# An eighth 2 MB weight slot for the experts, two output buffers instead of three, one buffer of gathered rows, and two reused slots loaded by halves

## The reference, cut to what matters

```python
# router: each token takes the 2 best of 8 experts of the best of 8 groups (64 experts)
order = jnp.argsort(eid)                      # 1024 assignments, sorted by expert
hid = jax.nn.silu(xb @ w1[e]) * (xb @ w3[e])  # w1, w3: 1024 x 512 in f32, 2 MB each
y   = hid @ w2[e]                             # w2: 512 x 1024 in f32, 2 MB
y_assign = y_slots[dest] * s_gate[:, None]    # each row by its gate, summed by token
```

## Time and profile before

| | |
|---|---|
| runs | 3236.83, 3237.40, 3237.57 us; median 3237.4 |
| profiled execution | span 3237.6 us from first to last instruction; the time of the runs is this same quantity, with nothing to add around it |
| PE busy / DVE / ACT / POOL | 95% / 43% / 28% / 6% of the span |
| mean granted clock of TensorE | 0.985 of full speed |
| HBM read / written | 600.30 MB / 18.90 MB |
| experts' loads on SP's queue | 7 names of slots, 2048 KB each, first issued at 2212.9 us, last at 3179.9 us |

### The profile page before, as it was taken

How to read it: one execution, slowest core, us unless ns; L and a number is a source line. 1 busy time by engine, 2 the same in 40 slices (tenths; PEclk the granted TensorE clock), 3 DMA queues, 4 the chain that set the end, 5 groups by cost and what they waited for, 6 DMA issues and landing times.

```text
span 3237.6 us, 35048 instructions
## 1 busy us (share of the span) xinstructions
PE 3082.8 (95%) x14831; PEld 2160.6 (67%) x14831; DVE 1377.5 (43%) x2276; ACT 890.4 (28%) x1429; POOL 194.1 (6%) x182
## 2 busy tenths in 40 slices
PE   9999999999999999999999999999999999999996
PEld 7668688887667778888888787888443344344342
DVE  5675543335486553333767665534311111111112
ACT  3453332232244332222244442322111111111111
POOL 0000000000000000000211010000100000000000
PEclk9999999999999999999999999999999999999998
DMA  5122222333222222323222121134999999999997
GB/s 181 53 79 91 66 91 89 101 108 121 66 66 91 79 77 86 104 93 115 86 85 69 62 98 59 59 104 166 406 429 430 430 431 429 429 430 430 430 429 304
DMA packets 192100, 611.07 MB, mean 189 GB/s; under 512 B 13396, under 2 KB 130932, under 8 KB 166976
## 3 DMA queue, kind: packets, MB, share of 16 engines
q1 hardware_dynamic: 177440, 585.65, 46.4%
q10 hardware_dynamic: 9056, 18.83, 1.7%
q0 software_dynamic: 5440, 4.27, 0.4%
HBM read 600.30 MB, written 18.90 MB: 191 GB/s over the span
## 4 chain that ended last, share of the span: by engine, by line
PE 84%; DVE 9%; ACT 3%; issue 2%; DMA 2%; POOL 1%; ACTq 0%; SPq 0%; POOLq 0%; DVEq 0%
PE bank L123 81%; PE bank L126 3%; DVE gate_acc L141 2%; DMA highs<-in_moe_w 1%; DVE probs L144 1%; DVE aprobs L144 1%; DVE x_tok L141 1%; ACT probs L129 1%; DVE qs L138 1%; DVE piece_rounded L138 0%; POOL root L138 0%; ACT piece_high_rounded L129 0%; DVE stat L156 0%; DVE small L135 0%; ACT xT_low_rounded L129 0%
## 5 line engine op out<-in xcount | busy, mean ns | idle before, releaser
L138 DVE TENSOR_TENSOR piece_rounded<-piece,piece_high_rounded 128x2048 fp32r<-128x2048 f32 (+2 forms) x160 | 346.8, 2171 | 526.3 <-ACT piece_high_rounded L129 526.1
L123 PE MATMUL bank<-xT_rounded,piece_high_rounded 128*128 128x512 f32 (+1 forms) x1424 | 542.0, 381 | 9.6 <-DVE piece_rounded L138 4.9
L123 PE MATMUL bank<-xT_low_rounded,piece_high_rounded 128*128 128x512 f32 (+1 forms) x1424 | 539.2, 379 | 0.0
L123 PE MATMUL bank<-xT_rounded,piece_rounded 128*128 128x512 f32 (+1 forms) x1424 | 539.0, 379 | 0.0
L138 DVE TENSOR_TENSOR gate_and_hidden<-gate_and_hidden,bank 64x512 f32<-64x512 f32 x64 | 69.2, 1082 | 762.4 <-ACT gate_and_hidden L129 762.4
L129 ACT ACTIVATE piece_high_rounded<-piece 128x2048 fp32r<-128x2048 f32 (+2 forms) x160 | 288.1, 1804 | 254.5 <-DMA piece<-in_ffn_w_down 102.4
L123 PEld LDWEIGHTS bank<-xT_rounded,piece_high_rounded 128*128 128x128 f32 x1424 | 270.0, 190 | 61.7 <-DVE piece_rounded L138 5.5
L123 PEld LDWEIGHTS bank<-xT_rounded,piece_rounded 128*128 128x128 f32 x1424 | 270.0, 190 | 49.2
L123 PEld LDWEIGHTS bank<-xT_low_rounded,piece_high_rounded 128*128 128x128 f32 x1424 | 270.0, 190 | 48.5
L123 PE MATMUL bank<-xT,xeT 128*64 128x512 f32 x496 | 237.2, 634 | 58.4 <-issue 57.9
L123 PE MATMUL bank<-tail_pair,xeT 128*64 128x512 f32 x512 | 244.9, 634 | 0.5 <-DVE extra L135 0.5
(11 more groups left out here) (350 smaller groups left out, 4832.1 us busy)
## 6 DMA issues: line engine op xcount, KB each, us to landing
tail_pair<-in_moe_w SPq DMA_DIRECT2D x32, 2048.0 KB, 21.8
highs<-in_moe_w SPq DMA_DIRECT2D x32, 2048.0 KB, 21.8
piece_high<-in_moe_w SPq DMA_DIRECT2D x31, 2048.0 KB, 17.3
xT<-in_moe_w SPq DMA_DIRECT2D x31, 2048.0 KB, 17.4
mT_pair<-in_moe_w SPq DMA_DIRECT2D x22, 2048.0 KB, 22.6
pieces<-in_moe_w SPq DMA_DIRECT2D x22, 2048.0 KB, 22.7
memory_norms<-in_moe_w SPq DMA_DIRECT2D x21, 2048.0 KB, 22.8
piece<-in_ffn_w_in SPq DMA_DIRECT2D x40, 1024.0 KB, 4.9
```

The costliest lines, as they stand in the source:

```text
L123: return self.engine.matmul(*a, **k) if self.engine is not None else Nothing()
L138: return self.engine.tensor_tensor(*a, **k) if self.engine is not None else Nothing()
```

## The change

`OUTS` goes from 3 to 2 and `rows` from two buffers to one. A slot `low`, released by the last gate product of the retention's merge, is put ahead of `tail`, so that eight pieces have a slot of their own (`FIRST_PIECES`). The pieces that take the first two reused slots, p8 and p9, are loaded by `load_first_reused`: the first halves of both when PE has done half of expert 0's upper products, the second halves when it has done the rest. Small tables of the router move to other places: `picks`, `rank`, `wide`, `both` and `local` to where `outs` and `ehidT` will be, so `out_act(0)` and `out_act(1)` wait for the mark `slots 1`; `e15` (and the slots' table in it) goes behind `xeT`.

```diff
-OUTS = 3
+OUTS = 2
+FIRST_PIECES = 8
...
-WORK = 119 * 256
+WORK = 120 * 256 + 32
...
         carve_from(0)
         self.outs = [carve(f"outs{j}", BANK) for j in range(OUTS)]
         self.ehidT = [carve(f"ehidT{j}", EH // P, CAP) for j in range(2)]
+        self.both, self.local = (carve(n, NT, EXPERTS) for n in ("both", "local"))
...
-        self.rows = [carve(f"rows{j}", D) for j in range(2)]
+        self.rows = carve("rows", D)
...
-        carve_from(WORK - 2 * SLOT)
+        carve_from(WORK - 4 * SLOT)
+        self.low_pair = carve("low_pair", 2 * SLOT)
         self.tail_pair = carve("tail_pair", 2 * SLOT)
...
+    def load_first_reused(self, e, n):
+
+        halves = []
+        for piece in (n, n + 1):
+            name, _, marks = self.slots[piece]
+            to, w, rows = self.expert_piece(piece), self.plan[piece][1], self.piece_rows(piece) // 2
+            halves.append((piece, f"piece_{name}_landed", marks, to, w, rows))
+        e.wait_ge(*self.at("half_used", 0))
+        for piece, landed, _, to, w, rows in halves:
+            e.dma_start(to[:, 0:rows, :], w[:, 0:rows, :]).then_inc(*e.lands(landed, "half_landed", piece))
+        for piece, landed, marks, to, w, rows in halves:
+            for mark in marks:
+                e.wait_ge(*self.at(*mark))
+            e.dma_start(to[:, rows:, :], w[:, rows:, :]).then_inc(*e.lands(landed, "landed", piece))
...
-        self.hidden_sum_pe(e, n, wg, wu, range(KD))
+        if n:
+            return self.hidden_sum_pe(e, n, wg, wu, range(KD))
+        self.hidden_sum_pe(e, n, wg, wu, range(KD // 2))
+        e.also("half_used", n)
+        self.hidden_sum_pe(e, n, wg, wu, range(KD // 2, KD))
...
+        self.add_slot("low", self.low_pair, ("pe", "m_gate", "retention", KD - 1))
         self.add_slot("tail", self.tail_pair, ("pe", "m_branch", "retention", KD - 1))
...
         if n >= OUTS:
             e.wait_ge(*self.at("stored", n - OUTS))
+        else:
+            e.wait_ge(*self.at("slots", 1))
         e.activation(self.outs[n % OUTS], self.bank("out", n)[:, :], ACT.Copy).then_inc(*e.tick("out", n))
...
+        reused = self.dense + FIRST_PIECES
         for n in range(2, len(self.plan)):
+            if n == reused:
+                self.load_first_reused(e, n)
+            if n in (reused, reused + 1):
+                continue
             self.load_piece(e, n)
```

## The result

| | before | after |
|---|---|---|
| median of the runs | 3237.49 us | 3251.52 us |
| profiled execution: run / span | span 3237.6 us | 3251.03 / 3249.2 us |
| first load into `mT` (the last merge is done) | 2247.89 us | 2256.66 us |
| from there to the end of the span | 989.7 us | 992.6 us |

The ratio is 1.0053 with a 95% interval of 1.0041 to 1.0064, so the kernel became slower by more than the 0.2% that can be told from no change, and it is outside the predicted range (3230.0 to 3243.0). Four of the six runs lie between 3248.62 and 3252.00; a fifth, 3268.04 at a mean clock of 0.938, lifts the ratio above that of the medians (1.0043), and the sixth, 6306.29, was disturbed and counts in the median of the table but not in the ratio (without it the median is 3251.03).

The account below looks back on a forecast made before the run. From 2373 us on, weight loads in a full DMA queue were taken to set the pace. A 7.4 us gain, nearly all paid back by PE's standstill (-0.3), plus 2.0 for the clock gave +1.7: 3239.1 us, range 3230.0 to 3243.0.

Parts of the forecast that it names:

- Moved tables: Router tables and the single `rows` buffer in the experts' stage: waits on `slots 1` end before they are asked, cost 0.
- the eighth slot: Extra slot `low`, loaded at about 2212.9 us while DMA stands idle: one load less in the full stretch, -4.97 us.
- ACT's copy of expert 2 waits for store 0: With two output buffers, `out_act(2)` waits from 2323.83 to 2340.18 us for store 0, some 16 us.
- PE stands ahead of `lower_pe(3)`: PE waits for ACT's `hidden_T_act(3)` before expert 3's lower products, from 2331.3 to 2341.2 us: 9.9 us.
- what the low clock takes behind it: PE's lowered granted clock after its wait before expert 3's lower products: 2.0 us lost, bounds 0 to 2.8.
- issue of p22: Weight load released by expert 5's upper products: issued at 2356.2 us, 9.9 us later than those products ended before, plus clock loss.
- hole behind the standstill: Load queue runs empty at 2352 to 2360 us, after PE's wait before expert 3's lower products: 4 to 8 us.
- first hole: Dip in loading at 2278 to 2282 us, where the first reused slot comes free: 2.4 us lost before, to be closed.
- PE's waits without a releaser, behind the hole: PE's waits for loads from 2373 us on, with no engine named as releaser: some 58 us, as before.
- The halves: First halves of p8 and p9 issued some 3.5 us earlier, during expert 0's upper products, to close the loading gap: -2.4 us.
- the rival with the full gain: Experts' stage: two output buffers suffice, stores stay hidden, late loads come 7.4 us earlier: 3230.0 us, 16 in 100.
- slower by the clock: PE's clock stays low through `lower_pe(3)`, gather and expert 5's upper products, 15 us more: 3252 us, 10 in 100.

Follow-up runs that it names:

- e1: The kernel before with only `WORK` raised from 119 * 256 to 120 * 256 + 32, moving `xT` by 1152 bytes: 3249.16 us, ratio 1.0036.
- e2: The changed kernel with `xT` allocated ahead of the work room, so the room's length no longer moves it: 3239.66 us, ratio 1.0006 to before.
- e3: The kernel before with two output buffers (`OUTS = 2`) and nothing else of the change: 3244.45 us, ratio 1.0020.
- e4: The changed kernel with the slots' index turned two experts earlier on PE and DVE, `xT` left at its new place: 3244.37 us, ratio 1.0024 to before.
- e5: The changed kernel with `xT` ahead of the room and the slots' index two experts earlier: 3231.31 us, ratio 0.9983 to before.
- e6: Same as e5, but p8 and p9 are loaded whole instead of in halves: 3231.69 us, ratio 0.9984 to before.
- e11: Same as e5, but without the slot `low`, so seven slots, with halves for p7 and p8: 3236.91 us, ratio 1.0003 to before.
- e9: The kernel before with a 128-byte pad ahead of the work room, moving the room and `xT` together: 3269.86 us (one run).

## Why the prediction was wrong, step by step

**The step that failed** is in "Moved tables", whose cost was put at nothing, together with the sentence on the eighth slot that `low` "leaves at about 2212.9 us, where `tail` left before". Both assume that nothing ahead of the experts changes. The longer room stood in the diff, and what it moves (`xT`, which 1424 triples of products stream and 320 hold as weights, by the page) was not costed. It costs 12.0 us (e1). No rival held it either: the one that ends slower put its price on the clock behind the standstill. That its time, 3252, is near the measured 3251.52 is chance.

**Step by step, shifted by the 8.8 us** by which after's stage begins later:

| step | forecast | measured |
|---|---|---|
| ACT's copy of expert 2 waits for store 0 | some 16 us | 16.7 us |
| PE stands ahead of `lower_pe(3)` | 9.9 us | 10.18 us |
| what the low clock takes behind it | 2.0 us | `lower_pe(3)` 5.18 instead of 3.65: 1.5 us |
| issue of p22 | 2356.2 + 2.0 = 2358.2 | 2366.90 - 8.8 = 2358.1 |
| hole behind the standstill | 4 to 8 us | 7.1 us |
| first hole | gone | 0.5 us left of 2.4 |
| PE's waits without a releaser, behind the hole | some 58 us | 51.7 us (24 times, from 2382 us on) |
| experts' stage, all in all | +1.7 us | +2.9 us (spans); +2.45 us by e2 |

The standstill, its cause, and that the queue then waits for PE are shown: e3 makes the standstill alone (+7.2), and e4 and e5 take it away by moving `slot_index` only (e5 against e2, e4 against the changed kernel).

**The halves** were costed at -2.4 us and bring nothing (e6, with both repairs). In the sum this did no harm, since what is gained ahead of p22 was worth nothing there; but the rival with the full gain was too large by it. Its true size is that of e5, some 6 us, all from **the eighth slot**, whose term (-4.97) held (5.6 to 6.7 by e11). The reason was in the prediction's own method: p22 was followed from slot to slot, but the loads between p8 and p21 were taken as a queue that stays full.

**The rival "slower by the clock"** did not come about: from 2348 to 2356 us, the end of the standstill included, the granted clock was 0.66 in the mean, and from 2356 to 2370 us it is 1.00 again.

**Open:** what in the chip makes a product slower when one of its operands is moved by 128 bytes, and whether the place itself counts or the place relative to the other operand. Moves of 128 and 1152 bytes are slow, of 512 and 1024 free; 256 bytes and moves under 128 were not tried.

## What to carry to other kernels

A line that only changes a size also moves everything allocated behind it; go through the addresses, not just the instructions, and keep what TensorE reads most at the place where it was measured to be fast (here `xT` ahead of the room, for 12 us). Before cutting a buffer, look for the first use, not the steady one: a store of 7.7 us was hidden nearly everywhere but at the start, where it waited for an index, and moving the index made two buffers enough. And a hole in a queue is worth filling only if the loads behind it aren't tied to releases that come no sooner; an extra slot moves them all by one load, an earlier half does not.

## What the runs showed of the hardware that was not expected

- A matrix product in f32 of 128 x 512 took 389 or 390 ns in the records at one place of its operands, and 391 to 395 ns when the streamed operand (`xT`) or the held one (`xT` in after, `hidT` in e9) was moved by 128 or 1152 bytes, at the full clock and with the same instructions; where `xT` and the whole room moved by 128, 1383 instead of 1414 products fit into 320 us, 2.2% fewer, and the kernel took 33 us more (e9, one run). Moves by 512 and 1024 bytes cost nothing.
- A load of 2 MB that met an empty queue landed 8.7 us after its issue in after, 8.1 in before.
